# Sparse attention: the outputs stay with features on partitions and are multiplied by a turned reciprocal

## What is computed

```python
def sparse_attend(q, k_sel, v_sel, valid):
    s = jnp.einsum('bqkgd,bqnkd->bqkgn', qg, k_sel).astype(jnp.float32) * (HEAD_DIM ** -0.5)
    s = jnp.where(valid[:, :, None, None, :], s, -jnp.inf)
    p = jax.nn.softmax(s, axis=-1).astype(v_sel.dtype)
    o = jnp.einsum('bqkgn,bqnkd->bqkgd', p, v_sel)
    return o.reshape(B, Q, ATTN_W)
```

## Time and profile before

| | us |
|---|---|
| median of 3 runs (lowest, highest) | 2797.74 (2795.54, 2804.0) |
| the profiled execution, its own time | 2784.8 |
| its span | 2782.8 |
| attention of the prompt, first score to last copy | about 966.5 to 1625.8 |
| busy in the span: PE, DVE, ACT, POOL | 2623.4, 1987.9, 1546.7, 849.7 |

### The profile page before, as it was taken

How to read it: one execution, slowest core, us unless ns; L and a number is a source line. 1 busy time by engine, 2 the same in 40 slices (tenths; PEclk the granted TensorE clock), 3 DMA queues, 4 the chain that set the end, 5 groups by cost and what they waited for, 6 DMA issues and landing times. The chain is left out here.

```text
span 2782.8 us, 46845 instructions
## 1 busy us (share of the span) xinstructions
PE 2623.4 (94%) x16259; PEld 1745.7 (63%) x16260; DVE 1987.9 (71%) x3025; ACT 1546.7 (56%) x2600; POOL 849.7 (31%) x1049
## 2 busy tenths in 40 slices
PE   8999999999999999999999978999989599999988
PEld 6766888988999845555466654555645355444433
DVE  4977943667995398788877637564444699999958
ACT  2134888843777567788888747311100156666636
POOL 3422433223333201234443231013130233333326
PEclk9999999999999999999999999999999599999999
DMA  3312433221444422200210368455451598888767
GB/s 122 113 46 69 147 106 116 64 73 54 140 140 120 159 80 80 65 20 28 84 39 21 92 190 259 167 178 185 141 193 42 223 348 318 349 305 314 278 220 286
DMA packets 241726, 415.59 MB, mean 149 GB/s; under 512 B 31284, under 2 KB 156988, under 8 KB 232586
## 3 DMA queue, kind: packets, MB, share of 16 engines
q1 hardware_dynamic: 176978, 252.38, 27.4%
q0 software_dynamic: 26160, 85.89, 9.2%
q10 hardware_dynamic: 38416, 75.08, 7.3%
HBM read 319.93 MB, written 97.44 MB: 150 GB/s over the span
## 5 line engine op out<-in xcount | busy, mean ns | idle before, releaser
L557 PE MATMUL p_ps_acc<-p_x_hi,p_w_hi 128*128 128x352 f32 (+2 forms) x1480 | 526.9, 356 | 2.5 <-DVE p_x_lo L861 2.5
L557 PE MATMUL p_ps_acc<-p_x_lo,p_w_hi 128*128 128x352 f32 (+2 forms) x1480 | 518.0, 350 | 0.0
L557 PE MATMUL p_ps_acc<-p_x_hi,p_w_lo 128*128 128x352 f32 (+2 forms) x1480 | 517.8, 350 | 0.0
L902 DVE SCALAR_TENSOR_TENSOR g_shared<-g_late,p_taps,g_shared 128x1024 f32<-128x1024 f32 x360 | 435.2, 1236 | 8.5
L557 PEld LDWEIGHTS p_ps_acc<-p_x_hi,p_w_hi 128*128 128x128 f32 (+1 forms) x1480 | 275.9, 186 | 51.0 <-issue 22.0
L3502 PE MATMUL e_ps_G<-g_late,e_xT 128*32 128x512 f32 x1312 | 303.0, 600 | 0.5
L3502 PE MATMUL e_ps_G<-l_wgu,e_xT 128*32 x656 | 298.1, 601 | 1.6 <-ACT e_xT L3566 1.5
L3502 PE MATMUL e_ps_G<-g_shared,e_xT 128*32 128x512 f32 x656 | 299.4, 601 | 0.1
L557 PEld LDWEIGHTS p_ps_acc<-p_x_lo,p_w_hi 128*128 128x128 f32 (+1 forms) x1480 | 276.1, 187 | 26.6 <-issue 0.5
L557 PEld LDWEIGHTS p_ps_acc<-p_x_hi,p_w_lo 128*128 128x128 f32 (+1 forms) x1480 | 275.6, 186 | 27.0
L480 POOL CAST p_w_hi<-g_late 128x1024 fp32r<-128x1024 f32 x74 | 98.0, 1324 | 597.4 <-PE p_ps_acc L557 578.7
(11 more groups left out here) (633 smaller groups left out, 5637.6 us busy)
## 6 DMA issues: line engine op xcount, KB each, us to landing
g_late<-in_w_in_dram SPq DMA_DIRECT2D x72, 512.0 KB, 4.2
l_wgu<-in_w_gate_dram SPq DMA_DIRECT2D x32, 1024.0 KB
l_wgu<-in_w_up_dram SPq DMA_DIRECT2D x32, 1024.0 KB
l_wd<-in_w_down_dram SPq DMA_DIRECT2D x30, 1024.0 KB
yb<-e_y ACTq DMA_DIRECT2D x41, 512.0 KB
featT<-p_stage ACTq DMA_DIRECT2D x28, 528.0 KB
featT<-p_stage ACTq DMA_DIRECT2D x28, 512.0 KB
g_late<-featT SPq DMA_DIRECT2D x54, 256.0 KB, 3.2
```

The lines of the kernel that those rows point to most:

```text
L557: m = nc.tensor.matmul(bank(n, tb)[0:rows, 0:width], wp[:, slot, k, 0:rows], xp[:, k, at], start=(k == 0 and i == 0), stop=(k == KD - 1 an ...
L902: ch.mark(nc.vector.scalar_tensor_tensor(dst, src, wt, dst, ALU.mult, ALU.add))
```

## The change

The outputs are no longer turned. Instead DVE takes the reciprocal of the sums spread over the 64 features of each head, 128 queries x 512 values (`invert`), PE turns that by four transposes (`turn_inverse`, U), ACT copies it to SBUF as `scale_T` (`keep_scale`), and DVE multiplies `ps_o` by it straight into the buffer that is stored (`normalise`). The buffer `oT_st` is single now and also holds the reciprocal, under the name `inv`. `invert` and U stand in the last slot of the tile itself, and `normalise` at the start of the next slot, ahead of its first `masked`. The letter O is gone from PE's table; V may now stand one slot later, written W. The tables of the background work are new.

```diff
-    0: "27.1 27.3 28.1 29.1",
...
+    0: "28.3 29.0 29.1 30.2",
...
-S0 T0 T1 O S1 V
...
+S0 W T0 T1 U S1 V
...
-T0 T1 V
+W T0 T1 U V
...
@@ attend_prompt
-        oT_st = ph.sb("oT_st", [P, 2, 4, P])
+        oT_st = ph.sb("oT_st", [P, 4, P])
+        inv = oT_st[:].rearrange("p j q -> p (j q)")
...
@@ SP
-                    sp.wait_ge(t_kept, at.kept[at.turns["o", t]])
+                    sp.wait_ge(o_done, t + 1)
...
@@ PE
-                def turn_raw(t):
+                def turn_inverse(t):
                     n = at.turns["u", t]
-                    pe.wait_ge(o_kept, t + 1)
+                    pe.wait_ge(inv_ready, t + 1)
                     bank_free(n)
                     for b in range(4):
-                        m = nc.tensor.transpose(ps_t[n % 3][:, b * P:(b + 1) * P], o_raw[:, t % 2, b, :], c.ident[:])
-                    m.then_inc(t_full, 1)
-
-                def turn_out(t):
...
+                        m = nc.tensor.transpose(ps_t[n % 3][:, b * P:(b + 1) * P], inv[:, b * P:(b + 1) * P], c.ident[:])
                     m.then_inc(t_full, 1)
 
                 def values(g):
                     t = g // 4
                     if g % 4 == 0 and t:
-                        pe.wait_ge(o_kept, t)
+                        pe.wait_ge(o_done, t)
...
-                            values(g)
-                turn_raw(NT - 1)
-                turn_out(NT - 1)
+                            values(g if part == "V" else g - 1)
@@ ACT
-                def keep_raw(t):
...
-                def keep_out(t):
...
+                def keep_scale(t):
+                    n = at.turns["u", t]
+                    if t:
+                        act.wait_ge(o_done, t)
                     act.wait_ge(t_full, n + 1)
+                    nc.scalar.copy(scale_T[:], ps_t[n % 3][:].rearrange("p (b q) -> p b q", q=P)).then_inc(t_kept, 1)
...
-                    if g % 4 == 0 and g:
-                        keep_raw(g // 4 - 1)
...
-                    if g % 4 == 1 and g > 4:
-                        keep_out(g // 4 - 1)
+                    if g % 4 == 3:
+                        keep_scale(t)
@@ DVE
+                def invert(t):
+                    dve.wait_ge(exp_done, 8 * t + 8)
+                    if t:
+                        dve.wait_ge(oT_stored[(t - 1) % 2], 64 * ((t - 1) // 2 + 1))
+                    nc.vector.reciprocal(inv.rearrange("p (h d) -> p h d", h=NH),
+                                         total[:, t % 2].rearrange("p j (x d) -> p (j x) d", d=1).to_broadcast([P, NH, HD])).then_inc(inv_ready, 1)
+
                 def normalise(t):
 
                     n = at.turns["u", t]
-                    dve.wait_ge(exp_done, 8 * t + 8)
-                    ch.link(nc.vector.reciprocal(inv[:, t % 2], total[:, t % 2]))
-                    dve.wait_ge(t_full, n + 1)
...
+                    dve.wait_ge(t_kept, at.kept[n])
+                    dve.wait_ge(pv_done, 8 * t + 8)
+                    nc.vector.tensor_tensor(oT_st[:], ps_o[:], scale_T[:], ALU.mult).then_inc(o_done, 1)
...
                 for g in range(NSLOT):
                     t = g // 4
+                    if g % 4 == 3:
+                        invert(t)
+                    if g % 4 == 0 and t:
+                        normalise(t - 1)
                     if g + 1 < NSLOT:
                         masked(g + 1, 0)
...
                         largest(g + 1)
-                    if g % 4 == 0 and t:
-                        normalise(t - 1)
```

More of the change, by code:

```diff
@@ L1154 @@
 COUNT_AT = {
[6 rows of a table removed]
[6 rows of a table added]
 }
 CHOOSE_AT = {
-    0: "27.1 27.3 28.1 29.1",
[L1164 to L1168, removed]
+    0: "28.3 29.0 29.1 30.2",
+    1: "31.2 39.4 40.4 41.4",
+    2: "43.5 43.5 44.5 45.5",
+    3: "46.2 48.4 49.3 49.5",
+    4: "53.1 53.5 54.0 54.3",
+    5: "55.4 55.5 56.5 57.2",
 }
 EARLY_CHOICE_AT = {
[L1171 to L1178, removed]
+    2: "16.2 16.4 16.4 17.2 17.3 17.3",
+    3: "18.4 20.2 21.2 22.0 24.0 25.5",
+    4: "12.2 13.3 14.0 14.3 15.2 15.3",
+    5: "1.1 5.1 8.5 9.2 9.2 9.4",
+    6: "1.4 2.0 2.1 2.3 3.0 3.2",
+    7: "0.1 0.1 0.2 0.5 1.0 1.1",
+    14: "3.5 4.3 6.1 7.2 9.3 9.4",
+    15: "9.5 10.1 10.2 11.2 11.4 12.1",
 }
-BRANCH_SLOTS = [0, 1, 2, 3, 4, 5, 6, 7, 8, 10, 11, 12, 14, 15, 18, 19, 23, 27, 31, 32, 33, 34, 35, 36, 37, 38, 39, 40, 41, 43, 44, 45]
+BRANCH_SLOTS = [0, 1, 2, 3, 4, 6, 7, 8, 9, 10, 12, 16, 17, 18, 20, 21, 22, 28, 31, 32, 33, 34, 35, 36, 37, 38, 39, 40, 43, 44, 45, 49]
 def places(text):
@@ L1249 @@
 TENSOR_ORDER = [row.split() for row in """
-S0 T0 T1 D0 D1 B V
-T0 T1 S0 V D0 D1 B
+S0 T0 T1 D0 V D1 B
+S0 T0 T1 D0 D1 B
+T0 S0 W T1 D0 V D1 B
+T0 S0 T1 U D0 D1 V B
+S0 T0 T1 D0 V D1 B
+S0 T0 T1 D0 D1 V
+S0 T0 T1 D0 V D1 B
+T0 S0 T1 U V D0 D1 B
+S0 T0 T1 B
+S0 W T0 T1 B
+S0 W T0 T1 B V
+S0 T0 T1 U V
+S0 T0 T1 B
+S0 W T0 T1
+S0 W T0 T1
+S0 W T0 T1 U
+S0 W T0 T1 B
+T0 W S0 T1 B
+T0 W S0 T1 B
+T0 W S0 T1 U V
+T0 S0 T1 B
+T0 W S0 T1 B
+T0 W S0 T1 B
+S0 T0 W S1 T1 U D0 D1
+W S0 T0 S1 T1 D0 D1 V
+S0 T0 S1 T1 D0 D1
+W S0 T0 S1 T1 D0 D1
+W S0 T0 S1 T1 U D0 D1 V
+S0 T0 S1 T1 D0 D1 B
+S0 W S1 T0 T1 D0 D1 V
+S0 T0 S1 T1 D0 D1 V
+S0 T0 T1 D0 D1 V U B
+T0 S0 T1 D0 V D1 B
 S0 T0 T1 D0 V D1 B
 S0 T0 T1 D0 V D1 B
-S0 T0 T1 U D0 V D1 B
-T0 T1 S0 O D0 V D1 B
+S0 T0 T1 D0 V D1 U B
+T0 S0 T1 D0 V D1 B
 S0 T0 T1 D0 V D1 B
[L1257 to L1291, removed]
-S0 T0 T1 S1 V
-S0 T0 T1 S1 V B
-S0 T0 T1 S1 U B V
-S0 T0 T1 S1 O B V
+S0 T0 T1 D0 D1 B
+S0 W T0 T1 U S1 B
+W S0 T0 T1 S1 V B
+S0 T0 T1 S1
+W S0 T0 T1 S1 V
+S0 T0 T1 S1 U B
+S0 W T0 T1 S1 V B
+S0 T0 T1 S1 B
+W S0 T0 T1 S1
+W S0 T0 T1 U S1 V
+S0 T0 T1 S1 V
+S0 T0 T1 S1 B
+S0 W T0 T1 S1 V
+S0 T0 T1 U S1 V
+S0 T0 T1 S1 V
+S0 T0 S1 T1
+S0 W T0 S1 T1
+S0 W T0 T1 U S1 V
+S0 T0 T1 S1
+W S0 T0 T1 S1 V
+S0 T0 T1 S1 V
+S0 T0 T1 U S1 V
 S0 T0 T1 S1 V
 S0 T0 T1 S1 V
[L1298 to L1306, removed]
-S0 T0 T1 O S1 V
[L1308 to L1312, removed]
-T0 T1 V
+S0 T0 T1 S1
+W T0 T1 U V
 """.strip().split("\n")]
@@ L1335, in __init__ @@
                         turn += 1
-                elif part != "V":
-                    key = {"U": ("u", t - 1), "O": ("o", t - 1), "B": ("c", BRANCH_AT.get(g))}[part]
+                elif part not in ("V", "W"):
+                    key = ("u", t) if part == "U" else ("c", BRANCH_AT[g])
                     self.turns[key] = turn
                     turn += 1
-        self.turns["u", NT - 1], self.turns["o", NT - 1] = turn, turn + 1
-        self.raw = {n: key[1] for key, n in self.turns.items() if key[0] == "u"}
         self.kept = {}
-        for n in range(turn + 2):
-            if n not in self.raw:
-                self.kept[n] = len(self.kept) + 1
+        for n in range(turn):
+            self.kept[n] = len(self.kept) + 1
     def use(self, unit, signals):
@@ L1595, in _ @@
                         elif part == "U":
-                            turn_raw(t - 1)
-                        elif part == "O":
-                            turn_out(t - 1)
+                            turn_inverse(t)
                         elif part == "D0":
@@ L1684, in _ @@
                 for g in range(NSLOT):
-                    if g % 4 == 0 and g:
-                        keep_raw(g // 4 - 1)
+                    t = g // 4
                     keep_turned(g, 0)
```

36 lines of the change are left out of this document (7 added, 29 removed), and 12 rows, old and new, of the table COUNT_AT.

## The result

| | before | changed |
|---|---|---|
| median of 4 runs, us | 2800.24 | 2834.63 |
| lowest, highest | 2795.54, 2804.0 | 2826.87, 2841.61 |
| ratio to before, 95% interval | | 1.0126 [1.011, 1.0143] |
| profiled execution, its span | 2784.8, 2782.8 | 2830.05, 2828.3 |
| the stage, first masked score to first transfer of the next stage | 661.5 | 689.6 |

The change makes the kernel slower by 34 us, or 1.3%. The stage is 28 us longer in the profile. What follows it took 1153 us in the profile before and 1171 after.

What follows compares the result with a forecast made beforehand. PE was taken as busiest, in a ring with DVE and ACT where place counts. Reciprocal 48, multiplication 7, less 7, 7.8, 4 and 0.8, gave +35 us: 2833 us against the median, range 2790 to 2860.

Steps and rivals of the forecast that it cites:

- The size of the reciprocal: On DVE, 128x512 values were to take 4.1 us, bounds 0.69 and 4.1, adding 62 us over 16 tiles.
- The share that passes: Of 62.6 us of later masked scores, 48 us were to reach the time, with bounds 15 and 63.
- the five late tiles: Delays after the first ten tiles, 20.8 us together; a share of 0.89 was to pass, 18.5 us.
- What goes, and the multiplication: PE's turn saves 7.8 us, ACT's copy 4, the stage's end 0.8; multiplication ahead of the masked scores costs 7.
- deferred values: V one slot later, W, in 28 of 64 slots: spares PE waits for ACT's last copy, 7 us.
- The new orders and places: PE's order and background work laid anew: 7 us for W, and part of why only 0.7 passes in ten tiles.
- The profile's signs: Reciprocal near 4.1 us, DVE some 62 us busier, PE 8 to 10 less, U waiting, ACT's maximum waits growing, 16 copies.
- the cheap reciprocal: Rival: the reciprocal takes 0.69 us on DVE and the kernel gains 11 us, 2787 us; chance 0.13.
- dear, but taken up: Rival: reciprocal 4.1 us, but new tables empty slots around it, only 15 us pass; 2791 to 2803 us; chance 0.15.
- it stacks: Rival: PE stands at U, all 62.6 us pass and the multiplication's 10.4 too; +64, 2862 us; chance 0.14.
- the rule of the Trainium skill: Reciprocal is an iterative divide with repeat count 8: an estimate of 4.3 us for 512 values, speaking against the change.
- this ring: Stage loop of scores (PE), mask and maximum (DVE), exponential (ACT), transposes (PE); work ahead of masked scores enters it.

Runs made afterwards that it cites:

- old_places_small: The kernel before's tables and places with the changed way of dividing, but a reciprocal of 8 sums and a spreading copy on DVE: 2813.2 us, ratio 1.0039.
- small_then_spread: The changed kernel, but DVE takes the reciprocal of the 8 sums and spreads it by a copy of 128x512: 2796.8 us, ratio to before 0.9983.
- multiply_later: small_then_spread with the multiplication behind the first masked scores of the slot instead of ahead of them: 2794.7 us, ratio to before 0.9975.
- reciprocal_later: The changed kernel with the wide reciprocal behind the slot's first masked scores, U behind the values, ACT's copy behind the exponentials: 2834.1 us, ratio to before 1.0111.
- one_more_reciprocal: The changed kernel with a second reciprocal of the same size ahead of the first, into a tile nobody reads: 2893.6 us, ratio to before 1.0332.

## Why the prediction was right

It forecast 2833 us, between 2790 and 2860, and slower with 0.72; measured were 2834.6. The direction and its cause were right, and were tested: the wide reciprocal by itself costs 55 us of stage in the kernel before, and without it the change is no loss. The near agreement of the sum is luck in part, since the terms below were off and cancelled. The sum of +35 was for the stage, which is 28 us longer in its profile; the timed medians differ by 34.

1. *The size of the reciprocal.* Estimated at 4.1 us from the slope between 8 and 17 values, measured 3.35 us. The extrapolation took the steeper slope, as if it grew with the width; from 17 to 512 values it is 6.2 ns a value. From one to 17 values it is 6.75, which would have given 3.6. Term: 62 us of DVE, in fact 50.
2. *The share that passes.* In slot 47 I let 3.7 of 4.8 us pass, because a wait of 2.1 us between the two pieces of the scores would shrink; only 0.73 us of these were idle, the rest was a count that DVE still has to do. 0.89 in the five late tiles and 0.7 in the ten first ones were taken, 48 us in all. Measured: 0.92 and 0.98 (39.0 of 42.3 us and 41.9 of 42.8), and all of 53.6 us in the kernel before. By these shares the reciprocal costs 46 to 50 us. The two errors cancel. The sum also had no term for the granted clock: some 13 us of the 39 to 42 are the same matmuls at a lower one.
3. *What goes, and the multiplication.* I counted 7.8 us less for the turn, 4 for the copy and 0.8 at the end, and 7 more for the multiplication ahead of the scores: together 5.6 us less. old_places_small has all of these and no deferred values, and its stage is 11 us longer; if its spreading copy passes in full, which no run shows, that is 3. This step failed by 9 us or more. The turn itself was spared as counted: in small_then_spread, at the clock of before, PE is busy for 607.1 us instead of 618.5. What isn't in the sum are waits: in old_places_small DVE is idle for 18.7 us ahead of the small reciprocals until an exponential ends, in 9 times, and for 10.8 us at the multiplication until the values are done, in 5 times. Which part costs, the place of the reciprocal, that of U or that of the multiplication, is open; multiply_later and reciprocal_later move these waits elsewhere and gain nothing clear.
4. *The new orders and places.* They got 7 us for the deferred values. Part of the 0.3 that was not to pass in the first ten tiles, 12.5 us, was laid to DVE's slack and to them, since background work might leave the slots of the reciprocal. Measured, they gain 22 to 25 us of stage with the new way of dividing (16 to 22 by the medians), and lose 6 with the old. The larger part of this gain was missed. Most of it is there without the wide reciprocal as well, so room made for that reciprocal is the smaller part, and what the rest comes from wasn't taken apart.
5. *The profile's signs.* DVE's busy time rose by 44 us in the stage (62 were forecast, by the larger reciprocal). PE's was to be 8 to 10 us lower and is 1.7 higher, 620.2 us instead of 618.5, with 64 matmul records less: the lower clock takes back what the turn gave. PE's weight loads wait for the reciprocal at U in 8 of the 16 slots, 13.8 us, and ACT has 16 copies for the outputs instead of 32. The waits of ACT for the negative maximum grew only from 34.8 to 37.3 us.

In sum, in stage time: reciprocal +47 to +50, the rest of the way of dividing +3, the places -22 to -25; together +28. The first two hold if the spreading copy's 8 us pass in full; if less passes, the reciprocal costs less and the rest more.

Of the rivals, the cheap reciprocal falls by its row; "dear, but taken up" is right in that the places win back 22 to 25 us, but not in that they hide the reciprocal; "it stacks" is right in its share and in that PE stands at U (13.8 us), and wrong in leaving out the places.

On the rule of the Trainium skill ("VectorE: DVE Perf Modes", "First, the fixed hardware budget", a repeat count of 8 for the reciprocal): the measurement gives (3352-266)/(512-17) = 6.2 ns for each further value, less than the 8.3 ns that 8 cycles at the page's clock make. What the prediction drew from the rule, a reciprocal several times dearer than a multiplication, agrees with the trace (3352 against 691 ns). Its number, taken as cycles per value, does not, and the measurement decides.

## What to carry over

Before a small operation is spread over a wide tile, look at its price per value in rows of two widths: here the spreading after the reciprocal costs 0.71 us, the reciprocal after the spreading 3.35, and that alone was the whole loss. In this ring, where PE has 6% of slack, four fifths or more of what was added to DVE passed on, ahead of the scores or behind them; the 79 us of waits for scores shrank by only 6 us when 50 us of work were put among them. And tables of places fit one set of costs: a change and its tables are measured together and apart, or a gain of the one hides the loss of the other.

## What was not expected of the hardware

The reciprocal on VectorE takes 3352 ns for 128x512 fp32 against 691 ns for a multiplication of that size, with a spread over 16 instances of 3348 to 3354 ns. A spreading copy from SBUF to SBUF of 128x512 took 506 ns in small_then_spread, where the multiplication that reads PSUM took 691.

Over the whole stage, TensorE's granted clock fell as its idle time grew. For the same 4540 matmul records it was 0.99 with 43.7 us idle (small_then_spread, busy for 607.1 us), 0.97 with 69.2 (changed, 620.2), and 0.93 with 115 (one_more_reciprocal, 641.4, with 4544 records). So a wait of PE cost more than its length here; that may be why one_more_reciprocal lost 64 us of stage for 53 us of work. Within the stage the two don't go together in every stretch, as the places 10 and 11 show.
